# The end of the last expert body in a one-core decoder layer: weights of the combination turned earlier, partial sums left open in PSUM, output stored by halves

## The reference, cut to what matters

```python
hg = jnp.einsum("nd,edf->nef", t, w_gate)
hu = jnp.einsum("nd,edf->nef", t, w_up)
act = jax.nn.silu(hg) * hu * gates[..., None].astype(t.dtype)
return jnp.einsum("nef,efd->nd", act, w_down).reshape(bt, s, d)
```

## Time and profile before

| what | value |
|---|---|
| median of 3 runs | 1140.29 us (1138.39 to 1141.09) |
| the profiled execution's own time | 1141.11 us |
| its span in the trace | 1139.2 us |
| granted TensorE clock, mean | 0.985 |
| PE busy | 1050.7 us (92%) |
| PEld (weight loads, beside PE) | 585.5 us (51%) |
| DVE busy | 550.0 us (48%) |
| ACT busy | 200.1 us (18%) |
| HBM read / written | 375.63 MB / 7.90 MB |

### The profile page before, as it was taken

How to read it: one execution, slowest core, us unless ns; L and a number is a source line. 1 busy time by engine, 2 the same in 40 slices (tenths; PEclk the granted TensorE clock), 3 DMA queues, 4 the chain that set the end, 5 groups by cost and what they waited for, 6 DMA issues and landing times.

```text
span 1139.2 us, 17257 instructions
## 1 busy us (share of the span) xinstructions
PE 1050.7 (92%) x7153; PEld 585.5 (51%) x7153; DVE 550.0 (48%) x1079; ACT 200.1 (18%) x457; POOL 41.7 (4%) x39
## 2 busy tenths in 40 slices
PE   8999999999999999999999998999997969787976
PEld 3687776666666676677777442333332313232322
DVE  3775554664455455495442135544443434343423
ACT  1022112221212231312010112121211111111110
POOL 0031010000100000010000000000000000000000
PEclk9999999999999999999999999999999999999997
DMA  9899449899999999724856368999999999999993
GB/s 327 329 287 323 185 142 417 319 372 348 350 409 390 375 358 361 295 97 158 336 201 243 148 267 356 417 425 426 427 427 428 427 429 429 427 429 427 427 427 135
DMA packets 38612, 384.53 MB, mean 338 GB/s; under 512 B 4863, under 2 KB 7551, under 8 KB 10207
## 3 DMA queue, kind: packets, MB, share of 16 engines
q1 hardware_dynamic: 35968, 375.83, 82.1%
q0 software_dynamic: 1568, 5.62, 1.9%
q10 hardware_dynamic: 1008, 2.10, 0.5%
HBM read 375.63 MB, written 7.90 MB: 337 GB/s over the span
## 4 chain that ended last, share of the span: by engine, by line
PE 71%; DMA 16%; DVE 8%; ACT 2%; issue 2%; POOL 1%; SPq 0%; ACTq 0%; DVEq 0%; POOLq 0%
PE ps L605 24%; DMA arena<-w_gu 12%; PE ps L597 7%; PE ps L1024 6%; PE ps L1001 5%; PE ps L1055 5%; PE ps L1039 4%; DMA arena<-w_proj 4%; PE ps L798 4%; PE ps L587 3%; PE ps L765 3%; DVE cst L1802 1%; PE ps L1060 1%; DVE cst L1741 1%; PE ps L781 1%
## 5 line engine op out<-in xcount | busy, mean ns | idle before, releaser
L605 PE MATMUL ps<-arena 128*128 128x256 f32 x1456 | 332.9, 383 | 1.0 <-DVE arena L1345 1.0
L605 PEld LDWEIGHTS ps<-arena 128*128 128x128 f32 x1456 | 270.5, 190 | 51.0 <-issue 14.4
L1024 PE MATMUL ps<-arena,cst 128*32 128x512 f32 x1024 | 122.8, 614 | 32.7 <-DMA arena<-w_gu 31.0
L1802 DVE STREAM_TRANSPOSE cst<-ps 128x512 f32<-128x512 f32 x31 | 22.2, 717 | 173.7 <-PE ps L1001 173.7
L597 PE MATMUL ps<-arena 128*64 128x256 f32 x832 | 101.3, 385 | 0.0
L1001 PE MATMUL ps<-arena,cst 128*32 128x512 f32 (+1 forms) x768 | 94.0, 603 | 0.0
L1024 PEld LDWEIGHTS ps<-arena,cst 128*32 128x32 f32 x1024 | 32.1, 112 | 118.2 <-issue 81.2
L1039 PE MATMUL ps<-arena,stat 128*32 128x512 f32 x512 | 66.6, 640 | 23.8 <-DVE stat L1806 23.8
L597 PEld LDWEIGHTS ps<-arena 128*64 128x64 f32 x832 | 55.1, 136 | 37.8 <-issue 14.2
L1824 DVE COPY arena<-ps 32x512 f32<-32x512 f32 x64 | 44.2, 691 | 45.8 <-PE ps L1039 44.5
L1055 PE MATMUL ps<-arena,cst 128*128 128x512 f32 x128 | 57.0, 598 | 9.4 <-ACT cst L1275 9.4
(11 more groups left out here) (264 smaller groups left out, 978.4 us busy)
## 6 DMA issues: line engine op xcount, KB each, us to landing
arena<-w_gu SPq DMA_DIRECT2D x64, 2048.0 KB, 29.2
arena<-w_dn SPq DMA_DIRECT2D x32, 2048.0 KB, 27.5
arena<-w_proj SPq DMA_DIRECT2D x43, 1024.0 KB, 7.7
arena<-kc SPq DMA_DIRECT2D x16, 2048.0 KB, 10.7
arena<-vc SPq DMA_DIRECT2D x16, 2048.0 KB, 9.4
arena<-w_o SPq DMA_DIRECT2D x16, 1024.0 KB, 4.9
arena<-kc SPq DMA_DIRECT2D x8, 1024.0 KB, 8.3
arena<-vc SPq DMA_DIRECT2D x8, 1024.0 KB, 9.8
```

Of the source, the lines that this page charges most:

```text
L605: last = mm(psum[:, regions(v)[j - 1]], left[a], right[:, a], start=first and opens and a == 0, stop=final and a == 1, skip_group_check=True)
L1024: last = mm(ps[g:g + 32, 0, :], xgT[:, s % 2, kt, :], w[:, k, :], start=kt < 4, stop=kt >= KT - 4)
```

## The change

Everything before the last body is the same. In the last body, with experts counted s = 0 to 7:

1. **Turns.** `early_turns` stands in expert 6 between its two pieces of gate/up weights. It turns `pw` into bank 4 (`pwT`), and columns 96 to 127 of `pw`, the weights of the last expert's 32 rows, four times into bank 5, once for each group of 32 partitions (`pw_last`). ScalarE copies both after the silu of expert 6.
2. **Products of 96 rows.** The rows of the first three experts of the half (96 partitions of `y4`) are multiplied for row tile 0 as four products into banks 4 to 7 that are left open (`start=True, stop=False`): the first before the last gate/up piece of expert 7, the second while ScalarE copies `part`, the others after the down products.
3. **Last 32 rows by groups.** ScalarE copies bank 3 whole to `y_last`. Four products of 32 rows, the n-th on partitions 32n to 32n+31, add the last expert's share to the four open banks.
4. **Third tile's sums in the bank.** `rows_first` puts `yres` of the third row tile into banks 1 and 0 with the identity, open, in two steps (before the last gate/up piece, and after the turned `part`). The last products of that tile (`last_tiles`, L1062 of the new file) add to them, so ScalarE copies the finished sum to `yres`, and VectorE's four adds go.
5. **Row tile 1** is computed last, into banks 2 to 5.
6. **Copies.** The last quarter of `y4` is copied from `y_last` in SBUF, two pieces each by ScalarE and VectorE.
7. **Stores.** Each row tile is stored in two halves of 1024 columns, in the order tile 0, tile 2, tile 1.

```diff
+        y_last = area(A_S, COLS)
+        pw_last = area(A_S + COLS, NT)
...
+            def store(t, h):
+                r0, m = ROWS[t]
+                cols = slice(h * D // 2, (h + 1) * D // 2)
+                sp.dma_start(o_y[r0:r0 + m, cols], yres[0:m, t, cols]).then_inc(y_stored_out, 16)
+            for h in range(2):
+                sp.wait_ge(added[0], last * 8 + (6 + 2 * h))
+                store(0, h)
+            for h in range(2):
+                sp.wait_ge(small_out, 2 * h + 2)
+                store(2, h)
+            for h in range(2):
+                sp.wait_ge(added[1], last * 8 + (6 + 2 * h))
+                store(1, h)
+            sp.wait_ge(y_stored_out, 96)
...
+            def early_turns(i):
+                pe.wait_ge(added[1], i * 8 + 4)
+                pe.wait_ge(added[2], i * 8 + 4)
+                pe.wait_ge(pw_made, i * 2 + 2)
+                for t, (r0, m) in enumerate(ROWS):
+                    last = tr(ps[:, 4, r0:r0 + m], pw[0:m, t, :], ident[0:m, 0:m])
+                last.then_inc(pwt_mm, 1)
+                for t, (r0, m) in enumerate(ROWS):
+                    for g in range(4):
+                        last = mm(ps[32 * g:32 * g + 32, 5, r0:r0 + m], pw[0:m, t, 96:128], ident[0:m, 0:m], start=True, stop=True)
+                last.then_inc(pwl_mm, 1)
+            def early_products(i, ns):
+                for n in ns:
+                    mm(ps[:, 4 + n, :], pwT[0:96, 0:P], y4[0:96, 512 * n:512 * n + 512], start=True, stop=False)
+            def rows_first(i, n):
+                for j in range(2):
+                    cols = slice(1024 * n + 512 * j, 1024 * n + 512 * j + 512)
+                    mm(ps[64 * j:64 * j + 64, 1 - n, :], ident[0:64, 0:64], yres[0:64, 2, cols], start=True, stop=False)
+            def last_tiles(i):
+                pe.wait_ge(yl_ready, 1)
+                for n in range(4):
+                    mm(ps[:, 4 + n, :], pw_last[32 * n:32 * n + 32, 0:P], y_last[32 * n:32 * n + 32, :],
+                       start=False, stop=True).then_inc(comb_mm, 1)
+                pe.wait_ge(ye_copied, i * (4 * BODY) + 4 * (BODY + 1))
+                for k in range(2):
+                    for j in range(2):
+                        cols = slice(1024 * k + 512 * j, 1024 * k + 512 * j + 512)
+                        last = mm(ps[64 * j:64 * j + 64, 1 - k, :], pwT[:, 2 * P:NT], y4[:, cols], start=False, stop=True)
+                    last.then_inc(small_mm, 1)
+                for n in range(4):
+                    if n >= 2:
+                        pe.wait_ge(added[0], i * 8 + (4 + n - 1))
+                    mm(ps[:, 2 + n, :], pwT[:, P:2 * P], y4[:, 512 * n:512 * n + 512], start=True, stop=True).then_inc(comb_mm, 1)
             def experts(i, first, final):
                 for s in range(BODY):
                     b = s % BATCH
+                    ends = final and s == BODY - 1
                     pe.wait_ge(xgT_ready, i * BODY + (s + 1))
                     for h in range(2):
+                        if final and s == BODY - 2 and h:
+                            early_turns(i)
+                        if ends and h:
+                            rows_first(i, 0)
+                            pe.wait_ge(pwl_ready, 1)
+                            pe.wait_ge(pwt_ready, i * 2 + 2)
+                            pe.wait_ge(ye_copied, i * (4 * BODY) + 4 * BODY)
+                            early_products(i, [0])
                         loaded(i, first, 3 * s + h)
                         w = gate_up(3 * s + h if first else 3 * s + h + 3 * BODY)
                         for k in range(KT // 2):
@@ -1026,10 +1090,14 @@
                         last.then_inc(piece_used, 1)
                     if not (final and s == BODY - 1):
                         gather((b + 1) % BATCH, i * 2 + (2 + (s + 1) // BATCH))
+                    if ends:
+                        early_products(i, [1])
                     pe.wait_ge(gu_copied, i * BODY + (s + 1))
                     for f in range(4):
                         last = mm(ps[:, 2, 32 * f:32 * f + 32], part[:, 128 * f:128 * f + 128], sel, start=True, stop=True)
                     last.then_inc(ht_mm, 1)
+                    if ends:
+                        rows_first(i, 1)
                     pe.wait_ge(act_ready, i * BODY + (s + 1))
                     loaded(i, first, 3 * s + 2)
                     w = down(3 * s + 2 if first else 3 * s + 2 + 3 * BODY)
@@ -1039,7 +1107,10 @@
                             last = mm(ps[32 * g:32 * g + 32, 3, :], actT[:, j, :], w[:, j, 512 * g:512 * g + 512],
                                       start=j == 0, stop=j == 1)
                     last.then_inc(piece_used, 1)
-                    if b < BATCH - 1:
+                    if ends:
+                        early_products(i, [2, 3])
+                        last_tiles(i)
+                    if b < BATCH - 1 or ends:
...
+            def experts(i, first, final):
                 for s in range(BODY):
                     b = s % BATCH
                     act.wait_ge(piece_used, i * (3 * BODY) + (3 * s + 2))
                     copy(part, ps[:, 0, :]).then_inc(gu_copied, 1)
                     act.wait_ge(ht_mm, i * BODY + (s + 1))
                     nc.scalar.activation(sg, ps[:, 2, 0:64], ACT.Silu).then_inc(silu_done, 1)
+                    if final and s == BODY - 2:
+                        act.wait_ge(pwt_mm, i * 2 + 2)
+                        act.wait_ge(pwl_mm, 1)
+                        copy(pwT, ps[:, 4, 0:NT]).then_inc(pwt_ready, 1)
+                        copy(pw_last, ps[:, 5, 0:NT]).then_inc(pwl_ready, 1)
                     act.wait_ge(piece_used, i * (3 * BODY) + (3 * s + 3))
+                    if final and s == BODY - 1:
+                        copy(y_last, ps[:, 3, :]).then_inc(yl_ready, 1)
+                        act.wait_ge(yl_ready, 1)
+                        for g in range(2):
+                            copy(y4[96:128, 512 * g:512 * g + 512], y_last[32 * g:32 * g + 32, :]).then_inc(ye_copied, 1)
+                        for n in range(2):
+                            act.wait_ge(small_mm, n + 1)
+                            for j in range(2):
+                                copy(yres[0:64, 2, 1024 * n + 512 * j:1024 * n + 512 * j + 512], ps[64 * j:64 * j + 64, 1 - n, :]).then_inc(small_out, 1)
+                        continue
...
+            def add_tile(ready, t, n, bank, before):
+                dve.wait_ge(comb_mm, ready)
+                cols = slice(512 * n, 512 * n + 512)
+                V.tensor_tensor(yres[:, t, cols], ps[:, bank + n, :], before[:, t, cols], ALU.add).then_inc(added[t], 1)
             def experts(i, first, final):
                 for s in range(BODY):
                     b, half = s % BATCH, s // BATCH
@@ -1819,6 +1911,14 @@
                         both(0, P).then_inc(scaled, 1)
                         dve.wait_ge(scaled, i * 8 + (4 * half + 4))
                         scale_rows(0, P).then_inc(p_made, 1)
+                    if final and s == BODY - 1:
+                        dve.wait_ge(yl_ready, 1)
+                        for g in range(2, 4):
+                            V.tensor_copy(y4[96:128, 512 * g:512 * g + 512], y_last[32 * g:32 * g + 32, :]).then_inc(ye_copied, 1)
+                        for t in range(2):
+                            for n in range(4):
+                                add_tile(i * 20 + (10 + 4 * t + n + 1), t, n, 4 - 2 * t, yres)
+                        continue
                     dve.wait_ge(piece_used, i * (3 * BODY) + (3 * s + 3))
                     for g in range(2, 4):
                         V.tensor_copy(y4[32 * b:32 * b + 32, 512 * g:512 * g + 512], ps[32 * g:32 * g + 32, 3, :]).then_inc(ye_copied, 1)
@@ -1827,9 +1927,7 @@
                     before = hres if first and half == 0 else yres
                     for t in range(2):
                         for n in range(4):
-                            dve.wait_ge(comb_mm, i * 20 + (10 * half + 4 * t + n + 1))
-                            cols = slice(512 * n, 512 * n + 512)
-                            V.tensor_tensor(yres[:, t, cols], ps[:, 4 + n, :], before[:, t, cols], ALU.add).then_inc(added[t], 1)
+                            add_tile(i * 20 + (10 * half + 4 * t + n + 1), t, n, 4, before)
```

More of the change, by code:

```diff
@@ L352, in hybrid_step @@
         added = [sem(f"added{t}") for t in range(3)]
+        pwl_mm, pwl_ready, yl_ready, small_mm, small_out = (sem(n) for n in ("pwl_mm", "pwl_ready", "yl_ready", "small_mm", "small_out"))
         NORM_X, NORM_MEM = 0, 3
@@ L567, in _ @@
             pieces(last, 3 * BODY - 10)
-            for t, (r0, m) in enumerate(ROWS):
-                sp.wait_ge(added[t], last * 8 + 8)
-                sp.dma_start(o_y[r0:r0 + m, :], yres[0:m, t]).then_inc(y_stored_out, 16)
-            sp.wait_ge(y_stored_out, 48)
+            def store(t, h):
[12 more added lines that the diff above has]
+            sp.wait_ge(y_stored_out, 96)
```

(8 more changed lines are left out.)

## The result

| | before | changed |
|---|---|---|
| median, same chip | 1140.64 us (6 runs) | 1133.89 us (6 runs) |
| profiled execution / its span | 1141.11 / 1139.2 us | 1134.82 / 1133.0 us |
| granted clock, mean | 0.985 | 0.993 |

The ratio is 0.9944 with a 95% interval of 0.9926 to 0.9963: faster by 6.4 us, 4 to 8. The forecast was 1134.0 us, in a range of 1131.0 to 1138.5.

What follows compares the result with a forecast made beforehand. Bound: the 27.4 us latency chain behind the last gate/up piece. Cumulative gains of 3.0 us (down products), 6.8 (last add) and 6.7 (span, with store queue) gave 1134.4, lowered to 1134.0 us; range 1131.0 to 1138.5.

Steps and rivals of the forecast that it cites:

- Turns and early products hidden: Before the gate/up pieces of experts 6 and 7: 2.5 us of turns and 1.8 us of products fit into idle.
- Clock held: Around the last gate/up piece: only 1.0 us idle before it, so full clock; down products 1.92 us for 3.68.
- -3.0 us in all: Cumulative gain at the down products' end: 1118.75 where it was 1121.74, including a start 1.25 us earlier.
- Order of the end: From the down products' end to the last add: bubble gone, fewer products and adds, 3.8 us gained.
- the sum's 0.86: Last 32 rows of tile 0: four products side by side take 0.86 us; in a row 3.43.
- the estimate of 1.12 us: Same four 32-row products, estimated from the Trainium skill's 3.07 times: 0.3 us more than the sum.
- Changes of form: Behind the last gate/up piece: seven changes between parts of the array, charged 0.13 to 0.15 us each.
- Queue of the stores: At the end: six stores move in order, 7.8 us of data from 1123.65 to 1131.5, landed 1132.1.
- A: Behind the last gate/up piece: clock falls for long, half speed to about 1123, time 1139.3 us; chance 0.09.
- C: TensorE stays at 1.2 GHz to the end of the new chain, time 1146 us, slower; chance 0.04.
- B: Final stores: halves of 4 KB a row all move at 200 GB/s, time 1139.6 us; chance 0.07.
- D: Early products wait for turned weights or copies, 1.8 us behind the last piece, 1136 us; 0.13 shared with short clock fall.

Runs made afterwards that it cites:

- e2_late: Changed kernel with the first row-placing pair and first 96-row product moved from before the last gate/up piece to behind it; 1136.68 us.
- e1_fill: Kernel before with two unused 128 x 512 products put into TensorE's wait for the last gate/up piece; 1138.48 us, ratio 0.9986.
- e6_nothird: Changed kernel without the stores of the third row tile; 1131.77 us, ratio 0.9926.
- e7_add3: Changed kernel with the third tile's sum made by four VectorE adds again, its row-placing products kept as filler; 1133.18 us, ratio 0.9947.
- e4_closed: Changed kernel without open banks for tile 0: four products over all 128 rows after y4's last quarter is copied; 1134.40 us, ratio 0.9958.
- e10_serial: Changed kernel with all four 32-row products taken from partitions 0 to 31; 1135.74 us, ratio 0.9965.
- e3_whole: Changed kernel with three whole stores (tiles 0, 2, 1) for the six halves; 1134.21 us, ratio 0.9962.
- e9_actq: Changed kernel with the third tile's two stores issued by ScalarE on its own queue; 1133.13 us, ratio 0.9941.

## Why the prediction was right, and where it was not

By its steps, as distances from the start of the last gate/up products (predicted, from 1111.82; measured):

| step | predicted | measured |
|---|---|---|
| turns in expert 6's wait | 2.5 us (0.8 to 4.1) | 1.4 us, hidden |
| down products start | +5.0 | +4.9 |
| down products end | +6.9 | +6.8 |
| last product ends | +15.2 | +15.3 |
| last add ends | +15.9 | +16.0 |
| stores' data | 7.8 us | 8.0 us |
| span ends | +20.7 | +20.9 |

- **Turns and early products hidden: right.** They fit in the waits; e2_late shows the price without cover.
- **Clock held: right in mechanism, for the executions that were traced.** e1_fill shows 2.9 us of it alone. What was mis-sized is its share against the median. The step "-3.0 us in all" up to the end of the down products is wholly clock, and is true of an execution in which the clock falls, as the profiled one of the kernel before. I took only 0.4 us off for that. By e1_fill's median the clock is worth 1.3 us over many executions (interval from a gain of 3.5 us to a loss of 0.5). Yet the median of the changed kernel lay where the sum put it, 4.6 to 5.9 us below e1_fill, where the distances give 3.6. The likely reason for that difference of 1 to 2.3 us is that e1_fill's profiled execution had the best clock of its twelve, so that its median holds less of the clock's gain than its profile; this was not shown. The landing of the last weights alone differs by 4 us between profiles, and its effect on medians of 6 to 12 runs was not separated either.
- **Order of the end, -3.8 us from the down products' end to the last add: right.** It is 12.8 us at e1_fill's full clock and 9.2 us now, 3.6. The 32-row products were side by side, as taken from the earlier trace rows, but 1.07 us in the chain, 0.2 more than the sum's 0.86; in a row at the 0.43 us that one takes they would be 3.43, 3.2 times as much. The Trainium skill (TensorE: Matmul & The Clock Gate, Part 3) gives 3.07 times for four such tiles; the trace agrees, and the estimate of 1.12 us from it was nearer than the sum's term.
- **Changes of form: right.** With 0.13 to 0.15 us each the sum met the last product to 0.1 us. The products behind a change of form start 0.1 to 0.2 us later than their predecessors' stream explains (L1044 starts 1.85 us after L1107, where products of the same form followed after 1.74). The trace agrees with the rule of the Trainium skill (TensorEngine Tiling, Key Properties) that a change drains the array; the cost is small. By the rows there are eight such places behind the last piece, not seven as the prediction counted.
- **Queue of the stores: right, and it is the new bound.** e6_nothird, e7_add3 and e4_closed show it from three sides; beyond about 2 us of delay the last add moves the end again (e4_closed, e10_serial). The halves are worth 1.0 us (e3_whole), most likely because the first store is issued 1.2 us earlier. The price of this bound: 1.6 us on VectorE (part 4 of the change) is worth only 0.2 us at the end.
- **Rivals.** A and C need a clock that falls; it did not in either profile of the changed kernel. The other runs have no trace. e2_late's profile shows that a long fall costs about 6 us, more than the 4.9 of rival A. B falls: 4 KB rows moved at 377 and 434 GB/s in full windows. D falls: no wait on `pwT`, `pw_last` or the copies shows.

## What to carry to other kernels

Work that is already possible belongs in a wait for data just ahead of the critical end, even if it is short: it takes length off the chain and may help to hold TensorE's clock. Look at the clock of all runs and not only of the one that was traced before you put a gain down to it. After such a change look for the next bound at once; here it is the store queue, and it hides 1.6 us of gain on VectorE. Read changes at the end of a program as distances from the last input's landing, since the landing scatters by 4 us, more than either part of the gain (2.9 and 3.6 us).

## What the runs showed of the hardware that I had not expected

- A busy TensorE can lose its clock. In e10_serial it fell to 0.50 at 1120.8, in a row of products on 32 partitions each that began at 1117.5, and TensorE had been busy for 5.89 of the 6 us from 1111. In e2_late it stayed at 0.50 for over 13 us while TensorE was busy with products on 32 to 128 partitions. Idle time alone does not decide either: 2.97 us before expert 6's second gate/up piece left the clock at 1.00 (before, e1_fill), 2.88 us before expert 7's did not (before, e2_late). What decides was not settled.
- One transfer of 2 x 64 x 512 elements used about two of 16 DMA engines (share 0.14, 53 GB/s) and cost 8.8 us at the end of the program; two of 64 x 512 did not.
- A second issuing queue for stores did not help: e9_actq was 0.5 us longer.
